# One decoder-layer step on one core: compression weights and position term moved beside the input projection, block queries beside the compression, and the samples' compressed attention joined with their main stage

## The chip, the cores and the metric

The kernel runs on one core of a Trainium2 chip. The metric is device time in microseconds (us) of one execution; runs are compared by their medians. Engines are named as the profile does: PE (TensorE matmul), PEld (TensorE weight load), DVE (VectorE), ACT (ScalarE), POOL (GpSimd), SP (SyncE).

## The reference, cut to what matters

One layer serves a prompt of 256 tokens and 8 samples of 8 new tokens each, with 1024 tokens of past. All is float32, D_MODEL is 2048.

```python
z = rmsnorm(x) @ w_in          # q, cmp k/v, sel k/v, win k/v, gates, u, v
# compress: raw keys or values in blocks of STRIDE = 16 rows, two blocks overlap
part = einsum('bnsgd,rsdh->brngh', sub, w1r) + einsum('rsd,rsdh->rh', pe, w1r)
kc   = silu(part[:, 0, 0:nc] + part[:, 1, 1:1 + nc]) @ w2
# attention to compressed keys; its probabilities choose blocks of the selected branch
o_cmp, p_cmp = gqa_attend(q, kc, vc, end <= q_pos)
idx   = top_k(blocks scored by sum of p_cmp over the heads of a group, 16)
o_sel = attend(q_rot, selected blocks);  o_win = attend(q_rot, last 512 keys)
o_nsa = gates[0] * o_cmp + gates[1] * o_sel + gates[2] * o_win
```

The term with pe is one vector of 128 numbers for the keys and one for the values: the position term. For a sample there are 16 past blocks and a current one, of which 16 are kept, so the kernel only finds the one block to drop (drop_add). After this come the prompt's attention, the output projection, the attention to a memory and a mixture of 16 experts; the diff touches none of these.

## The kernel before

The kernel is written engine by engine. A stage is a Block: each engine has its own list of instructions and waits on semaphores by hand, and no engine passes the end of a Block before all have reached it. An era (end_of_era) closes with a barrier too and clears the semaphores. Nothing is scheduled by a planner: the order in each list is the order of execution.

The input projection (lines 390 to 635) makes ten column tiles. TensorE multiplies tile n in three row groups (r = 0, 1 of 128 tokens, r = 2 of the 64 sample tokens), L519 and L523, from two weight buffers by turns; the even one lies in raw, the buffer into which GpSimd later gathers the cache. SyncE loads tile n when tile n - 2 is done (L462) and stores states behind that. ScalarE takes products out of PSUM (L566), VectorE rotates. The ninth tile is U1, the tenth GU (gates and the first part of u); behind it ScalarE does a gelu (L582) and the sigmoid of the gates (L583), and SyncE stores them to HBM. QQ and QR hold the queries of a tile until they are transposed.

The compression (lines 642 to 840) runs ten turns, keys and values of two samples each by turns, the last two for the prompt. In a turn ScalarE and VectorE regroup gathered rows (L769, raw to rawg), TensorE transposes them in eight blocks (L708), ScalarE and VectorE copy these out (L775, subT), and TensorE multiplies with w1 (L719, hidden), always eight blocks of the turn interleaved with the eight transposes of the next. ScalarE applies silu with the position term as its bias (L797), TensorE makes keys and values from it (L732, L735), VectorE keeps them. SyncE loads w1, the position rows, w2k and w2v at the start of the stage (L677 to L681). TensorE waits for all of these behind the first turn's transposes, transposes the position rows (L743), waits for VectorE, and sums the term in 32 matmuls, w1 as weights and one moving column (L748); the loop comes after. GpSimd gathers turn n's rows when turn n - 2's are regrouped (L248).

The samples' compressed attention (lines 861 to 927) is a Block of its own: SyncE loads the gates in 16 small DMAs; VectorE clears q_bd and qr_bd (L871, L872) and copies the queries in as diagonal blocks (L878); TensorE scores (L918), VectorE centres (L881 to L883), ScalarE takes the exp (L911), VectorE normalises (L885 to L887), TensorE sums over the heads (L922), VectorE finds the block to drop (L890 to L901) and multiplies by the gate (L903), TensorE transposes (L926), VectorE copies (L906).

The samples' main stage (lines 930 to 1161) then loops over the samples. SyncE reads eight page numbers into registers and loads keys, then values (L978, L979). TensorE transposes the keys in six groups (L999, turn_keys), copied by ScalarE and VectorE in turns (L1059), and scores them (L1012, L1015); VectorE takes the scores (L1118), finds maxima (L1122) and normalises (L1131); ScalarE does the exps (L1068). Ahead of the loop stand turn_keys(0), scores(0), turn_keys(1).

## Time and profile before

| what | value |
|---|---|
| three runs | 1887.93, 1881.65, 1880.87 us; median 1881.65 |
| the profiled execution's own time | 1877.32 us |
| its span in the trace | 1875.5 us |
| its mean granted clock of TensorE | 0.907 |
| busy | PE 83%, PEld 43%, DVE 21%, ACT 16%, POOL 4% |
| to 414.85 us | start, memory's projection, input projection |
| 414.85 to 616.26 us | compression and the passage to it |
| 616.26 to 659.61 us | samples' compressed attention, first keys |
| 659.61 to 839.6 us | samples' loop, at 0.98 of the clock |
| 839.6 us to the end | all other stages |

The span goes from the first to the last instruction of one execution. The clock is the share of full speed (2.4 GHz) that was granted; 0.50 is 1.2 GHz. A float32 matmul has two records in the trace, a transpose one. Line numbers are those of the kernel before.

### The profile page before, as it was taken

What the parts mean: (1) busy time and instruction counts of PE and PEld (TensorE: products, weight loads), DVE (VectorE), ACT (ScalarE), POOL (GpSimd) and SP (SyncE); (2) the same over time, 40 slices, a digit from 0 to 9 for tenths busy, and PEclk for the clock granted to TensorE, in tenths of its full rate; (3) what the DMA queues carried; (4) which work ended last, traced back from release to release, by engine and by line L of the source; (5) the groups of instructions that cost most, each with busy time, mean ns of one, the idle gap of its engine ahead of it and who ended that gap; (6) DMA issues with size and microseconds to landing.
All of it is one profiled execution on the core that took longest, in us unless ns stands there. A gap on an engine that the chain in (4) does not pass through costs nothing. (4 is left out here: it accounts for less than half of the span.)

```text
span 1875.5 us, 17915 instructions
## 1 busy us (share of the span) xinstructions
PE 1564.6 (83%) x6791; PEld 811.9 (43%) x6791; DVE 388.8 (21%) x765; ACT 293.0 (16%) x620; POOL 74.3 (4%) x107
## 2 busy tenths in 40 slices
PE   7999999987999378886769999967978878798880
PEld 4444445555556355563344456543323332233230
DVE  3101100001222343336541021351101010011014
ACT  3000000111222022225520002310000000000001
POOL 0000000000000000000000000000110101010100
PEclk9999999997999589996869999977998989899895
DMA  8463332423310054410057222468998999999955
GB/s 317 182 271 127 135 114 90 153 90 137 120 66 6 23 170 144 147 59 8 1 180 250 90 90 91 167 259 308 395 406 310 398 407 403 395 353 413 408 231 194
DMA packets 113799, 380.15 MB, mean 203 GB/s; under 512 B 17459, under 2 KB 55387, under 8 KB 83047
## 3 DMA queue, kind: packets, MB, share of 16 engines
q1 hardware_dynamic: 108050, 343.27, 48.7%
q0 software_dynamic: 5552, 27.89, 4.3%
q10 hardware_dynamic: 144, 8.26, 1.0%
q8 instruction: 36, 0.59, 0.1%
q14 instruction: 17, 0.14, 0.0%
HBM read 390.41 MB, written 26.49 MB: 222 GB/s over the span
## 5 line engine op out<-in xcount | busy, mean ns | idle before, releaser
L2194 PE MATMUL bank<-W,hT_e 128*64 128x512 f32 x576 | 277.6, 635 | 59.5 <-DMA w_u<-in_w_exp_up 58.6
L2195 PE MATMUL bank<-w_u,hT_e 128*64 128x512 f32 x576 | 277.6, 635 | 0.0
L2194 PEld LDWEIGHTS bank<-W,hT_e 128*64 128x64 f32 x576 | 81.4, 146 | 248.5 <-issue 161.8
L2211 PE MATMUL bank<-W,actT 128*64 128x512 f32 x576 | 143.9, 657 | 9.0 <-ACT actT L2222 9.0
L719 PE MATMUL bank<-subT,w 128*128 128x504 f32 (+1 forms) x320 | 134.5, 550 | 0.0
L519 PE MATMUL bank<-raw,hT 128*128 128x512 f32 (+1 forms) x320 | 131.6, 573 | 0.6 <-PEq L280 0.6
L519 PE MATMUL bank<-w_in,hT 128*128 128x512 f32 (+2 forms) x320 | 123.7, 547 | 0.0
L1588 PE MATMUL bank<-W,mixT 128*128 128x512 f32 x256 | 114.0, 606 | 1.6 <-DVE mixT L1809 1.6
L519 PEld LDWEIGHTS bank<-raw,hT 128*128 128x128 f32 x320 | 61.5, 193 | 67.8 <-issue 67.6
L519 PEld LDWEIGHTS bank<-w_in,hT 128*128 128x128 f32 x320 | 60.4, 190 | 61.1 <-issue 61.1
L2211 PEld LDWEIGHTS bank<-W,actT 128*64 128x64 f32 x576 | 44.0, 150 | 95.6 <-issue 90.2
L2240 DVE SCALAR_TENSOR_TENSOR act_w<-bank,row_w,gate 64x512 f32<-64x512 f32 x18 | 13.6, 757 | 334.0 <-ACT gate L2220 334.0
L2195 PEld LDWEIGHTS bank<-w_u,hT_e 128*64 128x64 f32 x576 | 81.4, 146 | 0.0
L1588 PEld LDWEIGHTS bank<-W,mixT 128*128 128x128 f32 x256 | 49.3, 194 | 63.8 <-issue 61.7
L719 PEld LDWEIGHTS bank<-subT,w 128*128 128x128 f32 x320 | 55.9, 207 | 33.1 <-issue 32.4
L2220 ACT ACTIVATE gate<-bank 64x512 f32<-64x512 f32 x18 | 10.6, 589 | 322.2 <-PE bank L2195 322.2
L708 PEld LDWEIGHTS bank<-const,rawg 128*128 128x128 f32 (+1 forms) x320 | 38.4, 145 | 44.6 <-issue 35.3
L708 PE MATMUL bank<-const,rawg 128*128 128x128 f32 (+1 forms) x320 | 45.8, 269 | 8.3 <-ACT rawg L769 8.3
L2172 POOL DMA_INDIRECT scratch_moe_y<-y,to_row x36 | 36.2, 1006 | 406.7 <-DVE y L2246 401.2
L1049 PE MATMUL bank<-v_in,pT 128*128 128x256 f32 x192 | 45.6, 387 | 7.2 <-ACT pT L1087 7.2
L999 PE MATMUL bank<-const,k_in 128*128 128x128 f32 x192 | 31.8, 312 | 22.6 <-DMA k_in<-in_cache_win_k 18.2
L2184 PE MATMUL bank<-const,rows_in 64*128 64x64 f32 x304 | 37.5, 277 | 15.1 <-DMA rows_in<-scratch_hn,from_row 15.1
(364 smaller groups left out, 1669.6 us busy)
## 6 DMA issues: line engine op xcount, KB each, us to landing
W<-in_w_exp_down SPq DMA_DIRECT2D x76, 1024.0 KB, 23.8
W<-in_w_exp_gate SPq DMA_DIRECT2D x72, 1024.0 KB
w_u<-in_w_exp_up SPq DMA_DIRECT2D x72, 1024.0 KB
raw<-in_w_in SPq DMA_DIRECT2D x3, 4096.0 KB
W<-in_w_out SPq DMA_DIRECT2D x3, 4096.0 KB, 13.5
w_in<-in_w_in SPq DMA_DIRECT2D x2, 4096.0 KB, 14.7
k_in<-in_cache_sel_k SPq DMA_DIRECT2D x64, 128.0 KB, 2.2
v_in<-in_cache_sel_v SPq DMA_DIRECT2D x64, 128.0 KB, 2.4
```

Of the source, the lines that this page charges most:

```text
L519: mm = pe.matmul(bank[4 * u + r][:, 0:width], hT[:, c, r * P:(r + 1) * P], w, start=(c == 0), stop=(c == KC - 1))
L708: mm = pe.transpose(bank[q % 4][:, g * n:g * n + n], rawg[0:n, q // 4, a:a + P], ident[0:n, 0:n])
L719: mm = pe.matmul(bank[4 + u][:, 0:heads * nk], w1[:, u, 8 * r + q, :], x[:, :, r:r + nk], start=(q == 0 and r == 0), stop=(q == 7 and r == 1))
L999: mm = pe.transpose(bank[4 + n % 2][:, k * P:k * P + P], k_in[:, 4 * m + k, c * P:c * P + P], ident)
L1049: mm = pe.matmul(bank[3][:, 256:256 + KVW], p, v, start=(n == 0), stop=(n == len(terms) - 1))
L1588: mm = pe.matmul(to, hT[:, c, r * P:r * P + P], w(c, slice(0, 512)), start=(c == 0), stop=(c == chunks - 1))
L2172: pool.indirect_dma_start(out=y_rows, out_offset=bass.IndirectOffsetOnAxis(ap=to_row[:, u, h:h + 1], axis=0), in_=y[:, u, h, :], in_offset ...
L2184: mm = pe.transpose(bank[6 + h][:, k * NS:k * NS + NS], rows_in[:, u, 8 * h + k:D:KC], ident[0:NS, 0:NS])
L2194: pe.matmul(bank[4 + u][0:NS, :], hT[:, u, c, :], w_g[:, c, :], start=(c == 0), stop=(c == KC - 1))
L2195: mm = pe.matmul(bank[4 + u][UP, :], hT[:, u, c, :], w_u[:, c, :], start=(c == 0), stop=(c == KC - 1))
L2211: mm = pe.matmul(bank[2 * u + n // 2][lane, :], actT[:, q, :], w_d[:, u, q, 512 * n:512 * n + 512], start=(q == 0), stop=(q == 3))
L2240: dve.scalar_tensor_tensor(out=act_w[UP, :], in0=bank[4 + u][UP, :], scalar=row_w[UP, bass.ds(turn, 1)], in1=gate[UP, :], op0=ALU.mult, op ...
```

## The change

The weights w1, w2k and w2v, the position rows and the term get their own scope ahead of the projection. Their loads are issued by SyncE behind the loads and stores that go with tile V1; QQ and QR now lie in the memory of w1. TensorE transposes the position rows behind tile UV and sums the term behind GU, the columns as weights (one wide) and w1 as the moving side, which gives a row; behind the last tile two one-column matmuls turn the rows into columns. GU becomes the ninth tile and U1 the tenth, with the gelu and sigmoid behind GU, and the gates' store has a semaphore of its own.

The compression has no wait for weights. SyncE loads the gates there, GpSimd clears q_bd and qr_bd ahead of its gathers, and VectorE fills them behind the regrouping in turn 2.

The Block of the compressed attention is gone; its instructions are spread over the lists of the main stage. SyncE's list there is as before.

```diff
+        w1_scope = top.enter_context(ExitStack())
+        right = lambda name, shape: w1_scope.enter_context(nc.sbuf_tensor(name, shape, F32, side="right"))
+        w1 = right("w1", [P, 2, KC, CH])
+        pe_rows, peT, pe_bias = right("pe_rows", [KC, 2, P]), right("peT", [P, 2, KC]), right("pe_bias", [P, 2])
+        w2k, w2v = right("w2k", [P, P]), right("w2v", [P, HD])
+        gates_stored = sem("gates_stored", True)
...
-            Q0, KS, Q1, KW, KC_, V2, V1, UV, U1, GU = range(10)
+            Q0, KS, Q1, KW, KC_, V2, V1, UV, GU, U1 = range(10)
...
+                        if n == V1:
+                            for u, kind in enumerate("kv"):
+                                sp.dma_start(w1[:, u, :, :], A[f"w_cmp_{kind}1"][0].rearrange("(m p) h -> p m h", p=P)).then_inc(cw_loaded, 16)
+                                sp.dma_start(pe_rows[:, u, :], A[f"pe_cmp_{kind}"][0].rearrange("(m l) d -> m (l d)", m=KC)).then_inc(cw_loaded, 16)
+                            for h in range(2):
+                                sp.dma_start(w2k[:, HD * h:HD * h + HD], A["w_cmp_k2"][0]).then_inc(cw_loaded, 16)
+                            sp.dma_start(w2v[:, :], A["w_cmp_v2"][0]).then_inc(cw_loaded, 16)
                     sp.wait_ge(v_ready, TILES)
                     store(out["sgu_v_s"][0].rearrange("b t n -> (b t) n"), Z[0:NS, 2, C_V:C_V + SW])
                     sp.wait_ge(gated, 1)
-                    store(scratch["gates"], Z[0:NS, 2, C_G:C_G + 48])
+                    sp.dma_start(scratch["gates"], Z[0:NS, 2, C_G:C_G + 48]).then_inc(gates_stored, 16)
                     sp.wait_ge(state_out, 16 * stored[0])
...
+                    def pe_terms():
+
+                        pe.wait_ge(cw_loaded, 16 * 7)
+                        for u in range(2):
+                            mm = pe.transpose(bank[3][:, 16 * u:16 * u + KC], pe_rows[:, u, :], ident[0:KC, 0:KC])
+                        mm.then_inc(pe_turned, 1)
+
+                    def pe_sums():
+                        pe.wait_ge(pe_copied, 1)
+                        for u in range(2):
+                            for m in range(KC):
+                                mm = pe.matmul(bank[7][0:1, P * u:P * u + P], peT[:, u, m:m + 1], w1[:, u, m, :], start=(m == 0), stop=(m == KC - 1))
+                        mm.then_inc(pe_summed, 1)
+
+                    def pe_columns():
+                        pe.wait_ge(pe_kept, 1)
+                        for u, row in enumerate((ta, tb)):
+                            mm = pe.matmul(bank[3][:, 64 + u:65 + u], row[0:1, :], cst("ones")[0:1, 0:1], start=True, stop=True)
+                        mm.then_inc(pe_made, 1)
+
                     for n in range(NT_IN):
                         multiply(n)
                         turn_blocks(n)
+                        if n == UV:
+                            pe_terms()
+                        if n == GU:
+                            pe_sums()
+                    pe_columns()
...
+                        if n == GU:
+                            act.wait_ge(taken_a, n + 1)
+                            act.activation(Z[:, :, C_U:GUV[1]], Z[:, :, C_U:GUV[1]], ACT.Gelu_apprx_tanh)
+                            act.activation(Z[:, :, C_G:C_G + 48], Z[:, :, C_G:C_G + 48], ACT.Sigmoid).then_inc(gated, 1)
                         copy_jobs(act, act.copy, 0, n)
-                    act.wait_ge(taken_a, NT_IN)
-                    act.activation(Z[:, :, C_U:GUV[1]], Z[:, :, C_U:GUV[1]], ACT.Gelu_apprx_tanh)
-                    act.activation(Z[:, :, C_G:C_G + 48], Z[:, :, C_G:C_G + 48], ACT.Sigmoid).then_inc(gated, 1)
 
...
+                    dve.wait_ge(pe_turned, 1)
+                    dve.tensor_copy(peT[:, :, :], bank[3][:, 0:32].rearrange("p (u m) -> p u m", u=2)).then_inc(pe_copied, 1)
+                    dve.wait_ge(pe_summed, 1)
+                    for u, row in enumerate((ta, tb)):
+                        ins = dve.tensor_copy(row[0:1, :], bank[7][0:1, P * u:P * u + P])
+                    ins.then_inc(pe_kept, 1)
+                    dve.wait_ge(pe_made, 1)
+                    dve.tensor_copy(pe_bias[:, :], bank[3][:, 64:66])
...
                     sp.dma_start(pages[:, :], A["page_table"].rearrange("b n -> (b n)").unsqueeze(0)).then_inc(pages_loaded, 16)
+                    sp.wait_ge(gates_stored, 16)
+                    for h in range(NH):
+                        sp.dma_start(gates_ht[h * NT:(h + 1) * NT, :, :],
...
                     sp.wait_ge(pages_loaded, 16)
+                    sp.wait_ge(gates_loaded, 16 * NH)
 
                 @block.gpsimd
                 def _(pool):
+                    pool.memset(q_bd[:, :, :, :], 0.0)
+                    pool.memset(qr_bd[:, :, :, :], 0.0).then_inc(bd_zero, 1)
...
-                    pe.wait_ge(cw_loaded, 16 * 7)
-                    for u in range(2):
-                        mm = pe.transpose(bank[7][:, 16 * u:16 * u + KC], pe_rows[:, u, :], ident[0:KC, 0:KC])
-                    mm.then_inc(pe_turned, 1)
-                    pe.wait_ge(pe_copied, 1)
-                    for u in range(2):
-                        for m in range(KC):
-                            mm = pe.matmul(bank[6][:, u:u + 1], w1[:, u, m, :], peT[:, u, m:m + 1],
-                                           start=(m == 0), stop=(m == KC - 1))
-                    mm.then_inc(pe_summed, 1)
                     for turn in range(TURNS):
...
+                    def blocks():
+                        dve.wait_ge(bd_zero, 1)
+                        for src, dst in ((qT, q_bd), (qrT, qr_bd)):
+                            for c in range(2):
+                                for h in range(2):
+                                    rows = slice(64 * h, 64 * h + 64)
+                                    a = (2 * c + h) * 32
+                                    dve.tensor_copy(dst[rows, c, :, a:a + 32].rearrange("p b (j t) -> p j b t", j=NJ),
+                                                    src[rows, 4 * c:4 * c + 4, 256:256 + NS].rearrange("p j (b t) -> p j b t", b=NB))
 
                     def keep(turn):
...
                             regroup(dve, dve.tensor_copy, 1, turn + 1)
+                        if turn == 2:
+                            blocks()
                     keep(TURNS - 2)
...
+                    for b in range(NB):
+                        for c in range(2):
+                            mm = pe.matmul(bank[6][:, NCS * b:NCS * b + NCS], q_bd[:, c, b, :], kcT[:, c, NCS * b:NCS * b + NCS],
+                                           start=(c == 0), stop=(c == 1))
+                    mm.then_inc(cmp_scored, 1)
                     turn_keys(0)
+                    pe.wait_ge(cmp_prob, 1)
+                    pe.matmul(bank[7][:, 0:NB * NCS], cst("group"), pc[:, :, :].rearrange("p b n -> p (b n)"),
+                              start=True, stop=True).then_inc(cmp_grouped, 1)
                     scores(0)
                     turn_keys(1)
+                    pe.wait_ge(cmp_gated, 1)
+                    for b in range(NB):
+                        mm = pe.transpose(bank[6 + b // 4][0:NCS, (b % 4) * P:(b % 4) * P + P], sc[:, b, :], ident)
+                    mm.then_inc(cmp_turned, 1)
...
+                    values(0)
+                    act.wait_ge(cmp_centred, 1)
+                    act.activation(pc[:, :, :], sc[:, :, :], ACT.Exp).then_inc(cmp_exp, 1)
                     copy_keys(act, act.copy, 0, 0)
-                    values(0)
                     copy_keys(act, act.copy, 0, 1)
...
                     queries(0)
-                    compressed(0)
+                    dve.wait_ge(cmp_scored, 1)
+                    own.link(dve.tensor_scalar(sc[:, :, :], bank[6][:, 0:NB * NCS].rearrange("p (b n) -> p b n", b=NB), SCALE, None, ALU.mult))
+                    own.link(dve.reduce_max(st[:, 0, :], sc[:, :, :], AX))
+                    dve.tensor_tensor(sc[:, :, :], sc[:, :, :], st[:, 0, :].unsqueeze(2).to_broadcast([P, NB, NCS]), ALU.subtract).then_inc(cmp_centred, 1)
                     copy_keys(dve, dve.tensor_copy, 1, 0)
+                    dve.wait_ge(cmp_exp, 1)
+                    own.link(dve.reduce_sum(st[:, 1, :], pc[:, :, :], AX))
+                    own.link(dve.reciprocal(st[:, 1, :], st[:, 1, :]))
+                    dve.tensor_tensor(pc[:, :, :], pc[:, :, :], st[:, 1, :].unsqueeze(2).to_broadcast([P, NB, NCS]), ALU.mult).then_inc(cmp_prob, 1)
+
+                    dve.wait_ge(cmp_prob, 1)
+                    dve.tensor_tensor(sc[:, :, :], pc[:, :, :], gates_ht[:, :, 0:1].to_broadcast([P, NB, NCS]), ALU.mult).then_inc(cmp_gated, 1)
+                    dve.wait_ge(cmp_grouped, 1)
+                    own.link(dve.tensor_copy(pg[:, :, :], bank[7][:, 0:NB * NCS].rearrange("p (b n) -> p b n", b=NB)))
+                    inner = pg[:, :, 4:4 * (NBLK - 1)].rearrange("p b (k r) -> p b k r", r=4)
...
                     queries(1)
                     copy_keys(dve, dve.tensor_copy, 1, 1)
+                    dve.wait_ge(cmp_turned, 1)
+                    for n in range(2):
+                        dve.tensor_copy(cmp_pT[:, 4 * n:4 * n + 4, :], bank[6 + n][0:NCS, :].rearrange("p (b r) -> p b r", b=4)).then_inc(cp_kept, 1)
+                    dve.wait_ge(cp_kept, 2)
+                    compressed(0)
                     normalise(0, 0)
```

Left out are most declarations, the old places of what is moved, the steps between the group sum and drop_add (L892 to L901, unchanged), and the removed Block, whose instructions are those shown as added, with bank 0 to 3 for 6 and 7.

## Rows read from the trace of the kernel before

**Rows 1.** By stage: length; busy PE, PEld, DVE, ACT, POOL; PEclk; DMA share; GB/s.

```profile
414.85:451.46 36.61, 19.07 (x98) 18.72 (x98) 4.19 (x6) 9.31 (x11) 0.94 (x1) 0.65 0.36 119
...
451.46:616.26 164.80, 163.94 (x691) 94.03 (x691) 37.64 (x61) 40.67 (x55) 4.68 (x5) 0.96 0.19 67
...
616.26:659.61 43.35, 11.10 (x43) 8.97 (x43) 14.82 (x30) 1.91 (x2) 0.00 (x0) 0.50 0.16 45
```

**Rows 2.** Timeline, SyncE in the projection: start us, duration us, engine, line, operation, tiles, count.

```profile
276.42 0.53 SPq L441 DMA_DIRECT2D out_cmp_v_s<-Z  x1
...
300.48 0.60 SPq L462 DMA_DIRECT2D w_in<-in_w_in  x1
```

**Rows 3.** Timeline at the projection's end (in brackets: idle before, and its releaser).

```profile
408.90 5.90 PE L523 MATMUL bank<-w_in,hT 128*64 128x210 f32 x64
...
414.84 0.67 ACT L566 COPY Z<-bank 64x210 f32<-64x210 f32 x2 [5.33 <-PE bank L523]
...
421.19 1.90 ACT L769 COPY rawg<-raw 128x2048 f32<-128x2048 f32 x1 [2.89 <-PEq L166]
```

**Rows 4.** Timeline at the start of the compression, TensorE.

```profile
423.14 5.07 PE L708 MATMUL bank<-const,rawg 128*128 128x128 f32 x32 [8.35 <-ACT rawg L769]
...
437.18 0.39 PE L743 MATMUL bank<-const,pe_rows 16*128 16x16 f32 x2 [8.97 <-DMA w2v<-in_w_cmp_v]
...
437.86 13.81 PE L748 MATMUL bank<-peT,w 128*128 128x1 f32 x64 [0.28 <-DVE peT L806]
...
458.42 1.86 PE L719 MATMUL bank<-subT,w 128*128 128x504 f32 x4
...
460.55 1.86 PE L719 MATMUL bank<-subT,w 128*128 128x504 f32 x4
```

**Rows 5.** Timeline at the compression's end: a matmul with 15-wide weights.

```profile
614.76 1.03 PE L735 MATMUL bank<-w2v,hid 128*15 128x64 f32 x8 [0.40 <-ACT hid L797]
```

**Rows 6.** Stretches of 2 us, with the granted clock, around the two changes of stage.

```profile
418.00:420.00 2.00, 0.00 (x0) 0.00 (x0) 0.00 (x0) 0.30 (x1) 0.00 (x0) 0.79 0.04 10
...
426.00:428.00 2.00, 2.00 (x20) 1.98 (x18) 1.31 (x2) 2.00 (x2) 0.00 (x0) 1.00 1.18 396
...
606.00:608.00 2.00, 2.00 (x14) 1.91 (x14) 0.23 (x1) 0.53 (x2) 0.00 (x0) 0.72 0.00 0
```

**Rows 7.** GpSimd's 1024-wide memset, and the regrouping copies (ns min/median/max).

```profile
L1569 POOL MEMSET mix<- x1: 956/956/956, 1140.5 to 1140.5; 128x1024 f32 x1
...
L769 DVE COPY rawg<-raw x10: 1204/1217/1228, 421.2 to 598.6; 128x2048 f32<-128x2048 f32 x8, 16x2048 f32<-16x2048 f32 x2
```

**Rows 8.** Timeline of the samples' compressed attention, to the first key transposes.

```profile
617.05 1.28 ACT L911 ACT_TABLE_LOAD   x1 [2.34 <-PEq L166]
...
624.07 7.08 PE L918 MATMUL bank<-kcT,q_bd 128*128 128x63 f32 x32 [8.27 <-DVE qr_bd L878]
...
633.99 0.68 DVE L885 TENSOR_REDUCE cmp_stat<-cmp_p 128x8 f32<-128x504 f32 x1 [0.69 <-ACT cmp_p L911]
...
635.67 2.05 PE L922 MATMUL bank<-cmp_p,const 128*128 128x504 f32 x2 [4.52 <-DVE cmp_p L887]
...
645.40 0.29 DVE L1103 COPY q_now<-qr_bd 128x256 f32<-128x256 f32 x1 [0.30 <-PEq L861]
...
651.11 4.03 SPq L978 DMA_DIRECT2D k_in<-in_cache_sel_k  x8
...
659.61 5.60 PE L999 MATMUL bank<-const,k_in 128*128 128x128 f32 x24 [15.83 <-DMA k_in<-in_cache_win_k]
```

**Rows 9.** Timeline of the first sample.

```profile
666.04 5.39 PE L1012 MATMUL bank<-keyT,q_now 128*128 128x512 f32 x12 [0.83 <-issue]
...
672.30 0.35 DVE L1118 SCALAR_TENSOR_TENSOR s<-bank,const 128x64 f32<-128x64 f32 x2 [6.36 <-PE bank L1015]
...
674.61 2.45 PE L999 MATMUL bank<-const,k_in 128*128 128x128 f32 x12 [2.35 <-DMA k_in<-in_cache_win_k]
...
680.86 5.39 PE L1012 MATMUL bank<-keyT,q_now 128*128 128x512 f32 x12 [1.09 <-DVE keyT L1059]
```

119 lines of the change are left out of this document (23 added, 96 removed).

## The prediction

> **What bounds the kernel now.** I read the page's slices first, then the table by stage, then the timeline at the three places that the diff touches, and last the granted clock in stretches of 2 us. The table [rows 1] shows what matters. From 451.46 to 616.26 the compression keeps TensorE busy for 163.94 of 164.80 us at clock 0.96: there only TensorE's work counts. Before and behind it lie two stretches in which no engine is busy: 36.61 us with TensorE busy 19.07 at a clock of 0.65, and 43.35 us with TensorE busy 11.10 at 0.50. These are chains of waits in which one engine works at a time. All three stages of the change meet there; the projection's own tiles are bound by TensorE, back to back to 414.80 [rows 3]. Stages are closed by barriers, and everything behind the first sample starts when its stage does, so time won here should stay won.
>
> **The end of the projection.** Now TensorE ends at 408.90 + 5.90 = 414.80, ScalarE takes the last tile until 415.51, then does the gelu, a table load and the sigmoid; it ends 2.89 us before 421.19, at 418.30, and the gates' store and the barrier fill the rest [rows 3]. After the change the gate tile GU is ninth and U1 last, so gelu, sigmoid and gates' store lie beside the 28 us of U1 on TensorE. The stage then ends with ScalarE's take at 415.51 (TensorE's two one-column matmuls and VectorE's bias copy run beside it, under 0.7 us together) plus a barrier. The barrier at the compression's end takes from 616.26 to 617.05 [rows 1, 8], 0.8 us. So the compression starts at 416.4 rather than 421.19: **-4.8 us**; not less than -3.8 if the bias copy comes last, not more than -5.3.
>
> **The position term.** Added to the projection are 2 transposes, 0.4 us by their row, and 32 matmuls with one-wide weights and 128 moving columns, two records each. No row has that shape. The nearest is L735 with 15-wide weights and 64 columns: 8 records in 1.03 us, about 0.11 each past the first, at the half clock [rows 5]; the narrow weights cost nothing beside the stream, so this is 64 columns x 2 cycles at 1.2 GHz. Then 128 columns at 2.4 GHz are 0.107 us, 64 of them 6.8 us; at half clock 13.7. The old form took 13.81 us at half clock, with 128-wide weights and one moving column [rows 4]. I take 6.8, since the projection's tile ahead runs at full clock: **+7.2 us** with the transposes. Lower end 6.8 (the stream cannot be shorter by that row), upper end 14.1 and 2.5 more if U1 starts slow. Its data: SyncE gets to the weight loads behind the last cmp store, at 277, and issues the next w_in load at 300.48 [rows 2]; the same loads, issued from 421.25 beside a gather, were all there at 437.18 [rows 4], 16 us. So they are in by 293, and TensorE asks for them behind UV, two tiles of 28 us behind 300.48. The w_in tile of V1 was issued ahead of them and the one of V2 waits until 300.48 in any case. The loads write over QQ and QR, which were last read for KW, two tiles earlier. Cost nothing; if that cover were gone, TensorE would pay up to 16 us.
>
> **The start of the compression.** Now the 32 transposes of the first turn run 423.14 to 428.21; then TensorE waits 8.97 us for the last weights, transposes the position rows, and multiplies until 451.67, at half clock; only then comes the loop [rows 4]. All this goes: the loop starts when the transposes are done, **-23.3 us** (451.5 to 428.2). What is late next? The copies of the first blocks and both regroupings of turn 1 are short of a step behind, so nothing. Then the clock. A step of the loop is 460.55 - 458.42 = 2.13 us [rows 4]; the first two took 458.42 - 451.5 = 6.9 instead of 4.26 because they began at half clock: 2.6 us more. In the stretch 426 to 428 the clock is 1.00 with only transposes running [rows 6], so a loop following at once starts at full clock: **-2.6 us**, bounds 0 and -2.6.
>
> **GpSimd's two memsets** go ahead of the gather of turn 2. A 1024-wide memset took 0.956 us [rows 7], so 2048 wide 1.9 and both 3.8. The gather then leaves some 2 us later relative to the stage; it is needed a turn later (8 x 2.13 = 17 us): nothing. VectorE's regrouping copy of 2048 elements (1.22 us [rows 7]) starts at the same moment. No row of before has the two engines at once. Lower bound 0. Upper: the copy waits for both memsets, 3.8 us, which its later blocks have half of: the fifth block's transposes come about 4.5 us into the stage, the copy would end at 5.0 and VectorE's first block copy follows: 1.2 us. I take **+0.3**, near the row without contention.
> The Trainium skill (SBUF — State Buffer, Who interferes with whom) says that such a copy and any GpSimd instruction exclude each other for a whole instruction. By it this term would be up to 1.2 rather than 0; no run here shows it yet.
>
> The eight copies of the block queries (under 3 us, between regroupings) lie behind turn 3's regrouping on VectorE; the copy queued behind them is wanted four steps later, 8.5 us: nothing. SyncE's 16 gate loads lie beside the loop: nothing.
>
> **The joined attention.** Now: stage at 617.05, memsets and copies on VectorE until TensorE's scores at 624.07, a chain over three engines to 645.40, then SyncE reads eight page numbers and issues the first keys at 651.11, 5.7 us later; they are there at 659.61 [rows 8]. After: SyncE does that from the barrier on, 617.05 + 5.7 = 622.8 and 8.5 more, so the keys K are there at 631.3 on the old clock: **-28.3 us**. TensorE's scores (7.08 us), VectorE's three steps and the exp come by 628, inside the wait. What comes back: VectorE copies the keys before it takes up the softmax, so behind its last key copy (0.1 ahead of 666.04, K+6.3) come sum, reciprocal and product, 635.67 - 633.99 = 1.7 us, then the group matmul (2.05 at half clock, 0.9 to 1.05 at full) [rows 8]. So the first sample's scores start at K+9.0 instead of 666.04 - 659.61 = K+6.4, and 2.6 us late are key_scored (K+15.3 for 672.30) and the second keys' copies, which wait for the same VectorE [rows 9]. The second transposes waited for a DMA until 674.61 = K+15.0, so their first blocks are hardly late, but VectorE sets their end. Then eight transposes (5.07/32 each [rows 4], 1.3 us), partly beside the last key copy: scores(1) at K+24.2 instead of 680.86 = K+21.25 [rows 9]. **+3.0 us**, bounds 2.6 and 6.3 (all at half clock). The drop-block chain is behind the group matmul and ahead of take(0,0): the old one with transposes and copies was 645.40 - 637.72 = 7.7 us, without those at most 6.4; scores(0) is 6.3: hidden. The copies of cmp_pT, 1.3 us, and normalise lie beside scores(1), 6.3 us: hidden.
>
> **The sum.** -4.8 + 7.2 - 23.3 - 2.6 + 0.3 - 28.3 + 3.0 = -48.5. The profiled execution took 1877.3 (span 1875.5); 1828.8 comes out. The median of the runs shown, 1881.65, is 4.3 above it; I carry that over: **1833 us**.
>
> **Rivals.** (A) *The sums run at half clock.* For it: the clock fell in 606 to 608 although TensorE was busy throughout, on narrow products [rows 6]. Against: those were paced by the loading of 128-wide weights; here nothing but the stream sets the pace. Price 6.9 + 2.5: 1842. (B) *The joined chain gives back more.* For it: three engines now carry two chains in their fixed order, and a late exp or a falling clock in TensorE's new gap of 2.4 us hits both; the clock did fall in the gap behind 414.80, to 0.79 in 418 to 420 [rows 6]. Against: each wait above has its cover. Price: 10 to 15 us of the 25: 1845. (C) *The loop still begins at half clock.* For it: TensorE stops for 3 to 4 us between the stages, and behind the stop at 414.80 the clock fell in 418 to 420; against it, the transposes brought it back [rows 6]. Price 2.6: 1836. (D) *Slower than before.* TensorE waits in its own order for the weights behind UV, and SyncE may be held by them so that the next w_in tile is late too. Small packets and a full queue speak for it (16 us for these loads, rows 4), the 80 us between issue and need against it. It costs only if the loads take over 80 us, and makes the kernel slower only beyond 128; at 132 it is 1885. (E) *The stages behind give it back*, because a transfer of theirs that starts early is the bound: 1881; against it, their loads are issued behind barriers.
>
> **How the numbers follow.** Forecast 0.65, A 0.12, B 0.11, C 0.06, D 0.03, E 0.03. The range takes the forecast with its bounds, 1823 (memset free, 2.6 of the clock kept, the median 4 nearer the profile) upward over C and A to 1846, and leaves half of B, D and E out. What a measurement can tell from no change is 0.5%, 9.4 us. Faster: forecast, A, B, C, 0.94. Within it 0.03, slower 0.03.
>
> **What would show it.** The profile after should have 64 records with 1-wide weights near 6.8 us in all; about 1.6 us between ScalarE's last take and the first regrouping; the loop's first product directly behind the first 32 transposes and its steps 2.13 us long from the start; no wait for w2v; SyncE's first key load 5.7 us behind the compression's barrier, and key transposes 8.5 us on; one new gap of about 2 us on TensorE behind them. It is wrong if the sums take 13 us, if the loop begins at half clock, if the keys come late, or if the stages from the first sample on grow by over 5 us.

## The result: 2.5% faster, and the profile after

The changed kernel took 1836.05 us (median of 4 runs, 1830.45 to 1837.16) for 1884.10 (4 runs, 1880.87 to 1887.93): ratio 0.9751, 95% interval 0.9718 to 0.9784, 41 to 53 us less. 1833 had been forecast. Timed again (6 runs beside 11 of the kernel before) the ratio was 0.9727 (0.9684 to 0.9771). Its first profiled execution took 1837.02 us with a span of 1835.2, 40.3 less than before's.

First the table by stage for the same three stretches as in [rows 1]: length, busy PE, PEld, DVE, ACT, POOL, clock, DMA share, GB/s.

```profile
422.30:431.22 8.92, 5.74 (x36) 5.66 (x37) 6.71 (x5) 5.36 (x6) 4.50 (x3) 0.81 0.11 11
431.22:593.73 162.51, 161.66 (x692) 93.09 (x690) 40.57 (x70) 41.94 (x58) 4.69 (x5) 0.97 0.23 81
593.73:609.00 15.27, 7.06 (x32) 6.90 (x32) 2.34 (x4) 2.31 (x3) 0.00 (x0) 0.50 0.43 134
```

The passage to the loop shrank from 36.61 to 8.92 us and the wait for the samples' first keys from 43.35 to 15.27; the loop itself from 164.80 to 162.51, at clock 0.97 for 0.96.

Now the timeline of the changed kernel at the end of the projection and the start of the compression (start, duration, instruction), which answers to [rows 3, 4, 7]. L563 is the sums with one-wide weights, L605 ScalarE's take of the last tile, L802 the regrouping, L753 the transposes, L764 the loop's first products.

```profile
386.56 7.15 PE L563 MATMUL bank<-w,peT 128*1 128x128 f32 x64
...
393.64 22.83 PE L533 MATMUL bank<-w_in,hT 128*128 128x420 f32 x64
...
422.34 0.69 ACT L605 ACTIVATE Z<-bank 64x210 f32<-64x210 f32 x2 [5.32 <-PE bank L537]
...
424.04 1.81 POOL L735 MEMSET q_bd<- 128x2048 f32 x1 [34.70 <-POOLq L166]
424.05 1.90 ACT L802 COPY rawg<-raw 128x2048 f32<-128x2048 f32 x1 [1.01 <-PEq L166]
424.08 4.60 DVE L802 COPY rawg<-raw 128x2048 f32<-128x2048 f32 x1 [1.05 <-PEq L166]
...
425.79 1.81 POOL L736 MEMSET qr_bd<- 128x2048 f32 x1
...
426.00 5.38 PE L753 MATMUL bank<-const,rawg 128*128 128x128 f32 x32 [3.18 <-ACT rawg L802]
...
431.22 1.86 PE L764 MATMUL bank<-subT,w 128*128 128x504 f32 x4
...
433.35 1.86 PE L764 MATMUL bank<-subT,w 128*128 128x504 f32 x4
```

The sums take 393.64 - 386.56 = 7.1 us. Behind the last product ScalarE has only its take and the barrier. The first products follow the transposes at once, and the second step comes 2.13 us after the first. Note VectorE's copy: 4.60 us for the 1.2 of [rows 7], while GpSimd runs two memsets.

The samples' start in the changed kernel, which answers to [rows 8, 9]: L986 the compressed scores, L943 the key loads, L964 the key transposes, L1036 VectorE's key copy, L1122 the sum of the softmax, L991 the group sum, L977 and L980 the scores, L997 the eight transposes.

```profile
594.55 7.06 PE L986 MATMUL bank<-kcT,q_bd 128*128 128x63 f32 x32 [1.26 <-PEq L166]
...
600.27 4.02 SPq L943 DMA_DIRECT2D k_in<-in_cache_sel_k  x8
...
609.00 5.43 PE L964 MATMUL bank<-const,k_in 128*128 128x128 f32 x24 [7.40 <-DMA k_in<-in_cache_win_k]
...
614.48 0.69 DVE L1036 COPY keyT<-bank 128x512 f32<-128x512 f32 x1 [0.87 <-PE bank L964]
...
615.08 0.67 DVE L1122 TENSOR_REDUCE cmp_stat<-cmp_p 128x8 f32<-128x504 f32 x1
...
616.76 1.49 PE L991 MATMUL bank<-cmp_p,const 128*128 128x504 f32 x2 [2.32 <-DVE cmp_p L1124]
...
618.04 6.68 PE L977 MATMUL bank<-keyT,q_now 128*128 128x512 f32 x12
...
624.56 1.00 PE L980 MATMUL bank<-kT,q_now 128*128 128x64 f32 x8
...
625.68 0.36 DVE L1097 SCALAR_TENSOR_TENSOR s<-bank,const 128x64 f32<-128x64 f32 x2 [4.12 <-PE bank L980]
...
630.60 2.66 PE L964 MATMUL bank<-const,k_in 128*128 128x128 f32 x12 [3.27 <-DVE keyT L1036]
...
633.05 1.72 PE L997 MATMUL bank<-const,cmp_s 128*63 128x128 f32 x8
...
634.60 5.32 PE L977 MATMUL bank<-keyT,q_now 128*128 128x512 f32 x12
```

The keys are there 8.7 us behind SyncE's first load, and TensorE's 7.06 us of compressed scores lie in the wait. Then TensorE has two gaps: it waits 2.32 us for the softmax until 616.76, which is new, and 3.27 us for a key copy until 630.60, since VectorE runs late by then. The kernel before had a gap of 2.35 us under the same key transposes, for a DMA [rows 9]. The granted clock, in stretches of 2 us (it stands behind the busy times), shows what the gaps cost beside their length:

```profile
426.00:428.00 2.00, 2.00 (x10) 2.00 (x11) 2.00 (x1) 0.59 (x1) 1.60 (x1) 0.56 0.11 2
...
430.00:432.00 2.00, 2.00 (x15) 1.60 (x14) 1.52 (x3) 2.00 (x3) 0.41 (x1) 1.00 0.65 124
618.00:620.00 2.00, 2.00 (x4) 0.93 (x3) 1.61 (x4) 0.00 (x0) 0.00 (x0) 0.50 0.82 241
622.00:624.00 2.00, 2.00 (x6) 0.94 (x5) 0.00 (x0) 0.00 (x0) 0.00 (x0) 1.00 0.95 312
632.00:634.00 2.00, 2.00 (x10) 1.86 (x10) 0.78 (x2) 1.75 (x4) 0.00 (x0) 0.50 0.00 0
```

At the start of the compression (426 to 432) it rises from 0.56 to 1.00 while transposes run, as in [rows 6]. In 618 and in 632 it is 0.50: each time behind a gap of TensorE, first under the first sample's scores, then under the second key transposes and the eight transposes. Only the first of these falls is new. Here are the kernel before's last products of the first sample (L1015, for L980) and its clock under the second key transposes:

```profile
671.27 1.00 PE L1015 MATMUL bank<-kT,q_now 128*128 128x64 f32 x8
```

```profile
676.00:678.00 2.00, 1.84 (x9) 1.44 (x9) 1.17 (x3) 0.59 (x1) 0.00 (x0) 0.50 0.98 326
```

Before, the first sample's scores took 671.27 + 1.00 - 666.04 = 6.23 us; now they take 624.56 + 1.00 - 618.04 = 7.52. From their end to the second sample's scores it is 9.04 us for 8.59.

### The profile page after: what moved, and what is told of

Read it like the earlier page. It is cut to its first block and busy times, and to the rows that moved or that the text cites. A ratio compares the mean times of both kernels' runs of the same rounds, so it can differ in the third digit from the quotient of the medians.

```text
span 1835.2 us, 17914 instructions
## 1 busy us (share of the span) xinstructions
PE 1567.1 (85%) x6795; PEld 806.7 (44%) x6795; DVE 389.2 (21%) x765; ACT 294.4 (16%) x621; POOL 78.1 (4%) x109
## 5 line engine op out<-in xcount | busy, mean ns | idle before, releaser
L2201 PE MATMUL bank<-W,hT_e 128*64 128x512 f32 x576 | 271.1, 625 | 51.4 <-DMA w_u<-in_w_exp_up 50.5
L2202 PE MATMUL bank<-w_u,hT_e 128*64 128x512 f32 x576 | 271.1, 625 | 0.0
L2218 PE MATMUL bank<-W,actT 128*64 128x512 f32 x576 | 160.8, 722 | 9.0 <-ACT actT L2229 9.0
L764 PE MATMUL bank<-subT,w 128*128 128x504 f32 (+1 forms) x320 | 132.5, 544 | 0.0
L533 PE MATMUL bank<-raw,hT 128*128 128x512 f32 (+1 forms) x320 | 131.6, 573 | 0.6 <-PEq L286 0.6
L533 PE MATMUL bank<-w_in,hT 128*128 128x512 f32 (+2 forms) x320 | 123.7, 547 | 0.0
L2218 PEld LDWEIGHTS bank<-W,actT 128*64 128x64 f32 x576 | 47.8, 164 | 109.1 <-issue 103.5
L533 PEld LDWEIGHTS bank<-raw,hT 128*128 128x128 f32 x320 | 61.5, 193 | 67.6 <-issue 67.3
L533 PEld LDWEIGHTS bank<-w_in,hT 128*128 128x128 f32 x320 | 60.4, 190 | 61.0 <-issue 61.0
L764 PEld LDWEIGHTS bank<-subT,w 128*128 128x128 f32 x320 | 55.3, 205 | 32.3 <-issue 31.6
L753 PEld LDWEIGHTS bank<-const,rawg 128*128 128x128 f32 (+1 forms) x320 | 38.4, 145 | 38.6 <-issue 34.7
L2253 DVE COPY y<-bank 128x512 f32<-128x512 f32 x18 | 12.4, 692 | 175.5 <-PE bank L2218 175.5
L977 PE MATMUL bank<-keyT,q_now 128*128 128x512 f32 x96 | 44.3, 612 | 6.2 <-DVE keyT L1036 5.4
```

The costliest lines, as they stand in the source:

```text
L533: mm = pe.matmul(bank[4 * u + r][:, 0:width], hT[:, c, r * P:(r + 1) * P], w, start=(c == 0), stop=(c == KC - 1))
L753: mm = pe.transpose(bank[q % 4][:, g * n:g * n + n], rawg[0:n, q // 4, a:a + P], ident[0:n, 0:n])
L764: mm = pe.matmul(bank[4 + u][:, 0:heads * nk], w1[:, u, 8 * r + q, :], x[:, :, r:r + nk], start=(q == 0 and r == 0), stop=(q == 7 and r == 1))
L977: pe.matmul(bank[n], q_now[:, c, :], keyT[:, c, 512 * n:512 * n + 512], start=(c == 0), stop=(c == 1))
L2201: pe.matmul(bank[4 + u][0:NS, :], hT[:, u, c, :], w_g[:, c, :], start=(c == 0), stop=(c == KC - 1))
L2202: mm = pe.matmul(bank[4 + u][UP, :], hT[:, u, c, :], w_u[:, c, :], start=(c == 0), stop=(c == KC - 1))
```

## The experiments

Twelve further profiles were taken. This table has for each kernel the stretches from landmark to landmark, in us: start of the compression; from there to its loop; the loop, to the last copy of the compression; to the first key transposes; from there to the second sample's scores; from the first key transposes to the end of the samples' loop; the prompt's attention; the experts, from the first load of w_exp_down to that of g_final; the span. The 305 us between the last two stretches (308.6 once) and the 38 to 41 behind them are left out.

| kernel | start | to loop | loop | to keys | keys to scores 2 | samples | prompt | experts | span |
|---|---|---|---|---|---|---|---|---|---|
| before | 421.2 | 30.3 | 164.7 | 43.4 | 21.3 | 180.3 | 100.6 | 590.9 | 1875.5 |
| before_again | 422.6 | 30.2 | 164.6 | 43.8 | 21.5 | 182.6 | 107.2 | 588.6 | 1887.3 |
| before_third | 422.6 | 30.4 | 164.6 | 43.6 | 21.5 | 182.4 | 104.8 | 593.3 | 1885.0 |
| after | 424.1 | 7.2 | 162.5 | 15.3 | 25.6 | 184.6 | 102.5 | 593.6 | 1835.2 |
| after_again | 425.9 | 7.2 | 162.6 | 15.0 | 25.6 | 184.5 | 102.5 | 593.7 | 1835.9 |
| weights_only | 423.4 | 7.2 | 162.7 | 43.1 | 22.3 | 181.4 | 107.7 | 588.3 | 1858.4 |
| join_only | 421.1 | 30.7 | 164.6 | 14.9 | 23.3 | 182.3 | 102.9 | 590.4 | 1850.0 |
| soft_first | 423.4 | 7.2 | 162.7 | 15.6 | 21.7 | 180.6 | 102.2 | 590.9 | 1827.3 |
| soft_again | 425.2 | 7.1 | 162.7 | 15.9 | 21.5 | 180.6 | 102.2 | 591.0 | 1829.1 |
| all_first | 424.9 | 7.0 | 162.7 | 16.0 | 20.9 | 181.6 | 104.5 | 593.9 | 1834.8 |
| sums_wide | 430.0 | 6.7 | 163.6 | 14.9 | 26.0 | 185.2 | 99.9 | 590.0 | 1834.5 |
| sums_back | 418.4 | 17.9 | 164.6 | 15.8 | 25.9 | 185.1 | 102.8 | 587.8 | 1837.2 |
| memset_after | 423.4 | 7.1 | 162.7 | 14.9 | 25.6 | 184.7 | 102.2 | 594.1 | 1832.7 |
| gates_last | 429.4 | 7.1 | 162.7 | 14.9 | 25.5 | 184.5 | 102.5 | 593.5 | 1839.2 |

**The two halves.** weights_only is the change up to the compression's loop; the attention is the old Block. join_only is the rest.

```diff
weights_only, against after
-                    pool.memset(q_bd[:, :, :, :], 0.0)
-                    pool.memset(qr_bd[:, :, :, :], 0.0).then_inc(bd_zero, 1)
...
-                        if turn == 2:
-                            blocks()
...
+            with nc.Block() as block:
+                @block.sync
+                def _(sp):
+                    sp.wait_ge(gates_stored, 16)
...
join_only, against before
+                    pool.memset(q_bd[:, :, :, :], 0.0)
+                    pool.memset(qr_bd[:, :, :, :], 0.0).then_inc(bd_zero, 1)
...
+                        if turn == 2:
+                            blocks()
...
```

> The projection's and the compression's part of the change alone: weights, position term and tile order as after, the compressed attention a stage of its own as before, with its own clearing and building of the block queries. Theory (the prediction's sum, corrected by the changed kernel's trace): the loop of the compression starts 20.3 us sooner and gains 2.2 more from a start at full clock, so the stage ends 22 to 23 us sooner than before, and the time is 22 to 24 us under before, half of the whole change. Rival: the two parts share a gain (a wait that either removes), then this part alone gives over 30 us. Rival: the join is where nearly all is won, then under 15 us.

> The other part alone: the block queries built beside the compression and the compressed attention spread over the samples' stage; weights, position term and tile order as before. Theory: keys of the first sample arrive 28 us sooner, the scores of the second sample start 24 us sooner, and the time is 23 to 25 us under before; the two parts add up to the whole change within the noise (46 to 49 us). The memsets on GpSimd lie at the same place and stretch VectorE's first regrouping copy from 1.2 to about 4.6 us, but the loop waits for the weights anyway, so it starts where it did. Rival: the parts share a gain, then over 30 us here; rival: what the join wins is given back in the samples' loop, then under 15.

Measured beside before's 1883.82: weights_only 1861.44 us, ratio 0.9892 (0.9852 to 0.9931); join_only 1853.36, ratio 0.9855 (0.9820 to 0.9889). By these medians weights_only is 22.4 us under before, as its theory had it, but join_only 30.5, above its 23 to 25 and on the line of its rival (over 30: a shared gain). At the end of the samples' loop, behind which come only stages that neither touches, the first is 22.2 us under before's first profile and the second 26.4; together 48.6, the whole change 46.4. Against the mean of before's three profiles at this point (842.4 us; they reach it at 839.9, 843.7 and 843.6) it is 53.6 for 48.0, and by medians 52.8 for 48.1, or for 53.7 in the second timing. So the halves add up within some 5 us, and by these figures a gain that both share is no larger; that there is none is not shown. One difference can be placed: join_only comes to its second sample's scores 23.3 us behind the first key transposes, the changed kernel 25.6.

```profile
639.35 5.31 PE L962 MATMUL bank<-keyT,q_now 128*128 128x512 f32 x12
```

```profile
640.00:642.00 2.00, 2.00 (x6) 0.83 (x5) 1.79 (x7) 0.00 (x0) 0.00 (x0) 1.00 0.84 250
```

The order of these instructions is the same in both, and so is TensorE's gap of 2.32 us ahead of the group sum (638.40), but the clock stayed at 1.00 behind it, so the group sum and the first scores ran at full clock. Otherwise each half gains where the theory put it: weights_only's loop starts 21.0 us sooner than before's (430.55 for 451.53), join_only's keys come 28.4 us sooner, and its first copy of 4.60 us costs the loop nothing that shows (30.7 us into the stage for 30.3).

**VectorE's order.** soft_first moves the softmax and the group sum ahead of the first keys, all_first the eight transposes and their copies too.

```diff
soft_first, against after
-                    turn_keys(0)
                     pe.wait_ge(cmp_prob, 1)
                     pe.matmul(bank[7][:, 0:NB * NCS], cst("group"), pc[:, :, :].rearrange("p b n -> p (b n)"),
                               start=True, stop=True).then_inc(cmp_grouped, 1)
+                    turn_keys(0)
                     scores(0)
...
-                    copy_keys(dve, dve.tensor_copy, 1, 0)
                     dve.wait_ge(cmp_exp, 1)
...
+                    copy_keys(dve, dve.tensor_copy, 1, 0)
                     dve.wait_ge(cmp_grouped, 1)
```

all_first also puts the eight transposes, in banks 2 and 3, ahead of turn_keys(0), their copies ahead of VectorE's copy_keys, and a wait for cp_kept ahead of scores(0).

> The changed kernel with the softmax of the compressed attention (sum, reciprocal, product, gate) ahead of VectorE's first key copies, and the sum over heads ahead of TensorE's first key transposes. Theory (the price of the join is VectorE's order, not the work): all of it then lies in the wait for the keys, the group sum is over before the keys come, the first sample's scores start about 6.4 us behind the keys' arrival as in the kernel before (9.0 after), and the second sample's scores some 2.6 us sooner than after; about 2.5 us under the changed kernel, which its time can hardly show. Rival: the work itself is the price (a late exp, TensorE's clock); then the group sum runs into the keys' arrival and nothing is won.

> As soft_first, and the eight transposes of the gated probabilities with their copies also ahead of the first keys (in banks 2 and 3, with a wait of scores(0) for the copies). Theory: the wait for the keys is 7.4 us long on TensorE and holds the group sum (2.0) and the transposes (2.0) nearly whole; the keys' transposes start at most 0.6 us later, and the second sample's scores start 3.5 to 4.3 us sooner than in the changed kernel. Time 3 to 4 us under the changed kernel. Rival: TensorE's transposes end too late and push the key transposes by 2 us or more; then it is no better than soft_first.

The timeline of soft_first from the group sum (L990) to the first sample's scores (L977):

```profile
605.68 2.05 PE L990 MATMUL bank<-cmp_p,const 128*128 128x504 f32 x2 [4.53 <-DVE cmp_p L1123]
...
608.82 5.31 PE L964 MATMUL bank<-const,k_in 128*128 128x128 f32 x24 [1.10 <-DMA k_in<-in_cache_win_k]
...
614.96 5.39 PE L977 MATMUL bank<-keyT,q_now 128*128 128x512 f32 x12 [0.83 <-issue]
```

The group sum is over ahead of the keys, and the scores come 6.14 us behind the key transposes' start instead of 9.04. At the second sample's scores the gain is 3.9 us, not 2.6: the first sample's scores ran at full clock (6.22 us for 7.52), so one of the two falls of the clock was gone. That is the distance of before (21.7 for 21.3 to 21.5): with this order the join costs nothing there. Of the 4.3 us that it cost in the changed kernel, 2.6 are the late softmax itself and 1.3 this fall, which does not follow from the order alone, as join_only has the same order without it. all_first wins 0.8 more at the second sample's scores, but runs these scores at half clock behind a gap of 1.08 us (7.03 us for 5.32):

```profile
631.47 7.03 PE L977 MATMUL bank<-keyT,q_now 128*128 128x512 f32 x12 [1.08 <-DVE keyT L1037]
```

Its samples as a whole take 0.9 more (181.6 for 180.6), so it is no better. In time: soft_first 1832.99, all_first 1835.01, both too near the changed kernel to tell.

**The sums of the position term.** sums_wide keeps their new place and takes the old form; sums_back takes old form and old place, and keeps only the early loads.

```diff
sums_wide, against after
-                                mm = pe.matmul(bank[7][0:1, P * u:P * u + P], peT[:, u, m:m + 1], w1[:, u, m, :], start=(m == 0), stop=(m == KC - 1))
+                                mm = pe.matmul(bank[7][:, u:u + 1], w1[:, u, m, :], peT[:, u, m:m + 1], start=(m == 0), stop=(m == KC - 1))
...
-                    pe_columns()
...
+                    dve.tensor_copy(pe_bias[:, :], bank[7][:, 0:2])
```

In sums_back the loads and TensorE's wait for them stay in the projection, and L742 to L750 of before stand again behind the first turn's transposes.

> The changed kernel with the sums of the position term in their old form at their new place: w1 as weights, 128 wide, and one moving column, still behind tile GU; the two turning matmuls at the end go. Theory (the stream of the moving side is the price, weights one wide cost nothing, and at full clock both forms are half as long as at half clock): the sums take 64 x 0.19 = 12 to 13 us instead of the 7.15 measured, and the compression starts 4.5 to 5.5 us later than in the changed kernel. Rival: the form doesn't matter, only the clock does; then about 7 us and the same start. Rival A of the prediction: the one-column form lets the clock fall behind the sums; then the first row group of tile U1 takes more than its 11.3 us.

> The changed kernel with only the loads of weights and position rows beside the projection; the transposes of the position rows and the sums are back in the compression, between the first turn's transposes and the loop, in their old form. Theory: the compression starts some 4.5 us sooner than in the changed kernel (419 to 420), since no sums lie in the projection and the gates' chain is hidden; then the loop waits for the sums alone. If TensorE's stop between the stages is under 4 us the sums run at full clock in 12 to 13 us, else at half in 13.8; the loop starts at 439 to 442 instead of 431.2, so 8 to 11 us are worth the place and form of the sums, and 10 to 12 the early loads. Rival: the wait for the loads was all of it, then the loop starts at 432 or sooner.

sums_wide's timeline: the sums, the next tile's products (L533), VectorE's copy of the term; and its clock before, in and behind the fall.

```profile
387.46 9.29 PE L563 MATMUL bank<-peT,w 128*128 128x1 f32 x64
...
396.61 25.82 PE L533 MATMUL bank<-w_in,hT 128*128 128x420 f32 x64
...
430.01 1.90 ACT L791 COPY rawg<-raw 128x2048 f32<-128x2048 f32 x1 [1.01 <-PEq L166]
```

```profile
390.00:392.00 2.00, 2.00 (x20) 2.00 (x19) 0.00 (x0) 1.98 (x3) 0.24 (x1) 1.00 0.62 246
392.00:394.00 2.00, 2.00 (x13) 2.00 (x13) 0.00 (x0) 1.59 (x2) 0.00 (x0) 0.61 1.02 434
...
394.00:396.00 2.00, 2.00 (x11) 2.00 (x11) 0.00 (x0) 0.00 (x0) 0.00 (x0) 0.50 1.02 434
```

The sums took 396.61 - 387.46 = 9.2 us, not 12 to 13. The expectation took the pace from the 0.19 us of one load's record, but the records overlap. At full clock one starts every 0.11 us (20 in the first stretch, those cut by its edges counted), which is the pace of the changed kernel's one-wide form too (64 in 7.1 us, 0.11 each); at half clock it is 0.21 (13.81 us for 64 in the kernel before). So all 64 would take about 7.1 us at full clock in either form, an estimate from that pace: the form by itself costs nothing. But the clock fell to 0.50 within them, and the first two row groups of U1 then took 25.82 us for 22.83. So the wide form costs 2.1 + 3.0 = 5.1 us, all of it by way of the clock, which is the shift of the start: 430.01 lies 42.55 behind the sums' start, 424.05 in the changed kernel 37.49. The rival of this run (the form doesn't matter, only the clock does) is right on the pace and wrong on the start. What rival A of the prediction feared happens with the wide form, and in no profile with the one-wide one. sums_back's sums and loop:

```profile
418.38 1.90 ACT L782 COPY rawg<-raw 128x2048 f32<-128x2048 f32 x1 [0.98 <-PEq L166]
...
426.59 9.80 PE L761 MATMUL bank<-peT,w 128*128 128x1 f32 x64 [0.66 <-DVE peT L829]
...
436.25 3.71 PE L733 MATMUL bank<-subT,w 128*128 128x504 f32 x4
```

Here the sums took 9.7 us and the clock fell again, so that the loop began at half clock (first step 3.71 for 1.86, loop 164.6 for 162.5). The loop starts 5.0 us later than in the changed kernel, and with the loop's 2.1 the compression ends 7.1 us later. Of both, 1.4 us are spread from ahead of the change: TensorE ended the ninth tile at 387.99 here and at 386.56 there. From that point the loop is 3.6 us later, and the compression's end 5.7. This is less than the 8 to 11 expected, since the sums, begun at full clock, are shorter than I had put them. The stage itself starts at 418.4, where 419 to 420 was expected. From the start of the stage the loop is 17.9 us away for before's 30.3: 12.5 us were the wait for the loads and the half clock that it left behind.

**GpSimd and VectorE at once.**

```diff
memset_after, against after
-                    pool.memset(q_bd[:, :, :, :], 0.0)
-                    pool.memset(qr_bd[:, :, :, :], 0.0).then_inc(bd_zero, 1)
                     for turn in range(2, NB):
...
                         gather_cmp(pool, turn)
+                        if turn == 2:
+                            pool.memset(q_bd[:, :, :, :], 0.0)
+                            pool.memset(qr_bd[:, :, :, :], 0.0).then_inc(bd_zero, 1)
```

> The changed kernel with GpSimd's two memsets behind the first gather of the compression instead of ahead of it. Theory (GpSimd's memset and VectorE's wide copy exclude each other): VectorE's first regrouping copy takes 1.2 us again instead of 4.6, the first gather is issued 3 to 4 us sooner, and the loop of the compression starts no more than 0.5 us sooner relative to its stage, since the blocks that need that copy come late. Rival: the 4.6 us are a cost of the stage's start (16 small gate loads beside it), then the copy keeps 4.6. Rival: the lock was on the path, then the loop starts 1 us or more sooner relative to the stage.

```profile
423.46 1.23 DVE L803 COPY rawg<-raw 128x2048 f32<-128x2048 f32 x1 [1.05 <-PEq L166]
...
426.58 1.81 POOL L740 MEMSET q_bd<- 128x2048 f32 x1
...
430.58 1.86 PE L765 MATMUL bank<-subT,w 128*128 128x504 f32 x4
```

The copy has its 1.23 us back with the 16 gate loads still beside it, the first gather is issued 3.2 us sooner (2.2 us into the stage for 5.4), and the loop's start behind the stage's is 7.14 us for 7.17. The lock is there and costs nothing here. The Trainium skill (SBUF — State Buffer, Who interferes with whom) calls it an exclusive hold for a whole instruction; the changed kernel's trace agrees and adds that the copy got no turn between the two memsets (4.60 us, to 1.1 behind the second's end).

**The order of the last two tiles.**

```diff
gates_last, against after
-            Q0, KS, Q1, KW, KC_, V2, V1, UV, GU, U1 = range(10)
+            Q0, KS, Q1, KW, KC_, V2, V1, UV, U1, GU = range(10)
...
-                        if n == GU:
+                        if n == U1:
                             pe_sums()
```

> The changed kernel with the order of the last two tiles undone: U1 ninth, with the sums behind it, and the gates' tile GU last, so gelu, table load and sigmoid again come behind the last product. Theory: the compression starts 2.5 us later than in the changed kernel (426.5), from ScalarE's chain of 2.8 us alone; the other 2 us of the 4.8 that the prediction gave the swap are the receipt of the gates' store, which no longer holds the stage. Rival: the swap is worth the whole 4.8, then 428.5 or more; rival: nothing, as TensorE's and VectorE's turning of the term ends last anyway, then 424.

```profile
424.77 1.13 ACT L621 ACTIVATE Z<-Z 128x1116 f32<-128x1116 f32 x1
...
427.20 0.32 ACT L622 ACTIVATE Z<-Z 128x144 f32<-128x144 f32 x1
427.55 0.49 SPq L506 DMA_DIRECT2D scratch_gates<-Z  x1
...
429.44 1.90 ACT L802 COPY rawg<-raw 128x2048 f32<-128x2048 f32 x1 [1.92 <-PEq L166]
```

The sums start at 388.28 in this profile and at 386.56 in the changed kernel's; with that taken off, the compression starts 3.7 us later, between theory and rival. ScalarE's chain from 424.77 to 427.52 is 2.8 of it, and 0.9 is the issue of the gates' store, which the barrier waits for (1.92 us idle for 1.01). The old 2.89 had 1.0 more; by the lists this is the store's receipt, for which SyncE waited there.

**The spread of what comes behind.**

> The changed kernel once more, to have it timed and profiled beside the two versions with the softmax ahead. Theory: the stretch up to the end of the samples' loop repeats its length within 1 us (46 us under before); what lay between there and the end of the span (6 us less gain than at that point in the first profile) is spread of stages that the diff doesn't touch: the prompt's attention (99.9 to 107.7 us in the profiles so far) and the experts (588 to 594), so this profile shows other lengths there, and its median is 46 to 49 us under before's. Rival: the loss behind the samples' loop belongs to the change; then both stages come out as in its first profile, 102.5 and 593.6, each time.

> The kernel before, profiled once more. The changed kernel's two profiles had the prompt's attention at 102.5 us and the experts at 593.6 both times, the only profile of before 100.6 and 591.0; these 5 us are what its profile gained less (40.3) than the stages of the change show (46.4). Theory: before's stages spread too, and this profile has other lengths there, up to 7 us more. Rival: 100.6 and 591.0 come again, then the 5 us belong to the change, by way of where the later stages stand in time or in memory.

> The same, a third profile of the kernel before: the same two expectations. With three profiles of it, a length that comes three times is the kernel's, one that differs is spread.

after_again's profile repeats the changed kernel's lengths (102.5 and 593.7), against its theory. But before's three profiles have 100.6, 107.2 and 104.8 us in the prompt's attention and 588.6 to 593.3 in the experts. The two rows are that stage in before_again and in soft_first:

```profile
843.73:950.93 107.20, 75.81 (x304) 40.09 (x304) 57.52 (x98) 50.49 (x165) 0.00 (x0) 0.68 0.02 5
```

```profile
789.46:891.66 102.20, 68.38 (x304) 36.17 (x304) 57.55 (x98) 50.38 (x165) 0.00 (x0) 0.77 0.02 6
```

The counts and VectorE's and ScalarE's busy times are the same; TensorE's clock is 0.68 in one and 0.77 in the other, for 5 us of length. before has 0.76 and 100.6, before_third 0.72 and 104.8. The first profile of before was its shortest one; the mean span of the three is 1882.6, that of the changed kernel's two 1835.6, 47.0 us less, as the timed runs have it. What remains open is why the changed kernel repeats these lengths so closely; in the table the two stages go with no one edit.

> The version with the softmax and the group sum ahead of the first keys, timed in more rounds beside the changed kernel. Theory: 3.7 us under the changed kernel, as the distance from the compression's end to the second sample's scores showed (37.2 for 40.9 us). Rival: lost in the spread of the later stages, no difference in the medians.

soft_again had 1830.28 us (median of 6) beside after_again's 1830.56, and 1829.1 for 1835.9 in the profile. The 3.9 us stand in both its profiles and in no median: single runs of one kernel lie 12 to 24 us apart here. It is the best version found by the traces; that it is faster was not shown by time.

## Why the prediction was right, step by step

- **End of the projection and position term**, +2.4 forecast: +2.9 (421.19 to 424.05). The sums took 7.1 us; their price by the 15-wide row and 2 cycles a column was 6.8. With their transposes at 0.3, the swap's -4.8 came out as some -4.5; the barrier cost 1.0 us here, where I had 0.8.
- **Early weights and no sums ahead of the loop**, -23.3 with +0.3 for the lock: -23.2. The loads were there in time; TensorE had no wait for them.
- **Full clock at the loop's start**, -2.6: -2.2. The transposes began at half clock (0.56) and brought it back, as in the old trace.
- **The keys 28.3 us sooner**: 28.1. This is the largest term and the simplest: SyncE's reading of page numbers no longer waits for a Block that it takes no part in.
- **The price of the join**, +3.0 forecast, +4.35 measured (21.25 to 25.60). The mechanism was right: VectorE copies keys first, the softmax late, and the first sample's scores start at K+9.04 for the K+9.0 of the sum. Mis-sized was the clock under these scores: I had them at full clock, 6.3 us, and behind the new gap of 2.32 us they ran in part at 0.50 and took 7.52, 1.3 us more than before. Behind them the sum was right within 0.2 (9.04 us to the second sample's scores, 8.9 in the sum). The half clock under the second key transposes is no part of the price, as the kernel before has it too.
- **Block queries, gate loads, memsets beside the loop**: nothing, as said.

The terms measured add up to -46.2 in the first pair of profiles for -48.5 forecast, and -46.4 stand at the end of the samples' loop. The profile's own gain, 40.3, was less by the prompt's attention (+1.9), the experts (+2.7) and the end (+1.4), which spread by more than that between executions. One sign of being wrong was met in that pair: the stages from the first key transposes on grew by 10.3 us (1215.9 to 1226.2), over twice the 5 allowed, 4.3 of them in the samples. Before's other two profiles have 1226.1 and 1223.9 there and the changed kernel's second 1225.2, so by the means the growth is 3.7, of which 2.8 are in the samples' stage, where a price had been forecast. That 1833 came so near to 1836.05 is in part luck, then: the stages gave 2.3 us less than forecast, and single runs lie further apart than that.

Rival A did not come true in this form, C and D not at all, and E is not borne out by the repeated profiles; of B the smallest part did, the fall of the clock in the new gap, 1.4 us.

## What to carry to other kernels

Look for stretches where one engine works at a time between two barriers, and ask of each chain which engine's first long step (here SyncE's page reads and loads) takes no part in it: letting that engine run ahead was worth more than any work saved. When two chains are joined in one engine's list, put the steps whose inputs are ready ahead of those that wait for a transfer; the other order cost its own length here (2.6 us) and, behind TensorE's gap, in six of the seven profiles with it some of the clock (1.2 to 1.6 us). A sum over the partitions of a matrix with one vector went at the same pace in both forms, but with the matrix as weights and one moving column the clock fell underway, and the products behind it paid too; with the vector as weights, one column wide, it did not, as long as the result may come out as a row.

## What the runs showed of the hardware

- 64 matmul records of 128 moving columns with one-wide weights: 7.1 us; 64 of one moving column with 128-wide weights: 9.2 us (sums_wide) and 9.7 us (sums_back), at a clock that falls from 1.00 to 0.50 underway, and 13.8 us when it was at 0.50 all along. At full clock both forms start a record every 0.11 us.
- VectorE's copy of 128 x 2048 float32 took 4.60 us instead of 1.23 beside two GpSimd memsets of 1.81 us each, in all nine profiles with the memsets in that place.
- The same prompt attention took 99.9 to 107.7 us, with the granted clock between 0.68 and 0.78.
- Behind the same gap of 2.32 us, with the same order of instructions, the clock fell to 0.50 under the first sample's scores in the changed kernel (7.52 us) and in five more profiles (7.4 to 7.8 us), and stayed at 1.00 in join_only (6.15 us). Why is open.
